# Stick-breaking attention: the mask and 1 - s move from VectorE to GpSimd, and the scores are made two units ahead

## The reference, cut to what matters

```python
def stick_breaking(q, k, v, q_pos, k_pos):
    """A[t,s] = sigmoid(z_ts) * prod_{s<j<t} (1 - sigmoid(z_tj)), s < t, in log space.
    q (B,T,H,d), k/v (B,S,H,d); swept in query blocks."""
    ...
        z = (jnp.einsum('bthd,bshd->bhts', qb, k) * scale).astype(F32)
        mask = k_pos[None, :] < pb[:, None]
        ln1m = jnp.where(mask, jax.nn.log_sigmoid(-z), 0.0)
        rc = lax.cumsum(ln1m, axis=3, reverse=True)
        excl = jnp.concatenate([rc[..., 1:], jnp.zeros_like(rc[..., :1])], axis=-1)
        a = jnp.where(mask, jnp.exp(jax.nn.log_sigmoid(z) + excl), 0.0)
        return jnp.einsum('bhts,bshd->bthd', a.astype(v.dtype), v)
```

## Time and profile before

| | us |
|---|---|
| median of 3 runs | 3688.18 |
| the three runs | 3682.5, 3688.18, 3698.48 |
| profiled execution | 3678.38 |
| its span, first to last instruction | 3676.8 |
| mean granted TensorE clock | 0.929 |

### The profile page before, as it was taken

One profiled execution on the slowest core, in us unless ns is written; L12 is line 12 of the kernel. 1 busy time (PEld: TensorE's weight loads), 2 busy tenths in 40 slices (PEclk: granted clock), 3 DMA queues, 4 the chain that ended last, 5 costly groups with the idle time before them and its releaser, 6 DMA issues. The chain is left out here.

```text
span 3676.8 us, 67694 instructions
## 1 busy us (share of the span) xinstructions
PE 3204.2 (87%) x25256; PEld 1989.8 (54%) x25256; DVE 1365.4 (37%) x3002; ACT 950.5 (26%) x1746; POOL 597.8 (16%) x1090
## 2 busy tenths in 40 slices
PE   6999987888998688799989998978889987887998
PEld 4556654555666455444455666545556654554443
DVE  3235086443224444312142350954433244442211
ACT  2012144332224333211020122433322242331110
POOL 0000000444010044400000000004440101452000
PEclk9999988999999799899989999989999997998999
DMA  5011103887120388710120011048861205995102
GB/s 175 18 36 33 50 10 105 265 287 244 38 83 1 117 278 290 249 66 16 46 96 28 28 45 44 1 129 288 284 217 33 72 1 173 295 299 186 57 29 72
DMA packets 268657, 439.67 MB, mean 120 GB/s; under 512 B 48818, under 2 KB 216403, under 8 KB 268339
## 3 DMA queue, kind: packets, MB, share of 16 engines
q1 hardware_dynamic: 205810, 239.96, 20.4%
q0 software_dynamic: 55744, 189.25, 15.6%
q10 hardware_dynamic: 6912, 7.87, 0.6%
HBM read 410.28 MB, written 26.65 MB: 119 GB/s over the span
## 5 line engine op out<-in xcount | busy, mean ns | idle before, releaser
L806 PE MATMUL ps<-W,xT 128*128 128x320 f32 (+7 forms) x5120 | 1482.9, 465 | 11.5 <-DVEq L449 11.5
L806 PEld LDWEIGHTS ps<-W,xT 128*128 128x128 f32 (+1 forms) x5120 | 856.7, 184 | 585.6 <-issue 291.5
L688 POOL DMA_DIRECT2D branch<-in_cache_sb_v_dram x480 | 258.8, 539 | 637.5 <-issue 597.3
L688 POOL DMA_DIRECT2D branch<-in_cache_fox_v_dram x480 | 258.9, 539 | 621.2 <-issue 579.6
L1468 ACT ACTIVATE branch<-ps 128x512 f32<-128x512 f32 x288 | 165.6, 595 | 386.6 <-PE ps L1051 378.2
L1051 PE MATMUL ps<-C,W 128*128 128x128 f32 x1280 | 199.4, 301 | 73.1 <-DMA W<-in_cache_fox_k_dram 26.6
L1051 PE MATMUL ps<-C,branch 128*128 128x128 f32 x1280 | 194.9, 295 | 65.7 <-DMA branch<-in_cache_sb_k_dram 18.0
L1136 PE MATMUL ps<-branch 128*8 128x64 f32 x9920 | 182.2, 234 | 55.9 <-DMA branch<-in_cache_fox_v_dram 27.6
L1073 PE MATMUL ps<-branch,work 128*32 128x512 f32 x896 | 229.9, 631 | 0.8 <-issue 0.2
L1051 PEld LDWEIGHTS ps<-C,W 128*128 128x128 f32 x1280 | 151.0, 151 | 141.0 <-issue 67.4
L1051 PEld LDWEIGHTS ps<-C,branch 128*128 128x128 f32 x1280 | 147.8, 149 | 146.3 <-issue 96.1
(11 more groups left out here) (246 smaller groups left out, 3389.1 us busy)
## 6 DMA issues: line engine op xcount, KB each, us to landing
branch<-in_cache_sb_v_dram POOLq DMA_DIRECT2D x480, 160.0 KB, 4.3
branch<-in_cache_fox_v_dram POOLq DMA_DIRECT2D x480, 160.0 KB, 4.1
W<-in_cache_sb_k_dram SPq DMA_DIRECT2D x248, 160.0 KB, 3.4
W<-in_cache_fox_k_dram SPq DMA_DIRECT2D x248, 160.0 KB
branch<-in_cache_sb_k_dram SPq DMA_DIRECT2D x240, 160.0 KB, 4.2
branch<-in_cache_fox_k_dram SPq DMA_DIRECT2D x240, 160.0 KB, 4.3
W<-in_w_in_dram SPq DMA_DIRECT2D x14, 1280.0 KB, 6.3
W<-in_w_in_dram SPq DMA_DIRECT2D x9, 1536.0 KB, 7.1
```

The costliest lines, as they stand in the source:

```text
L688: pool.dma_start(ringV[:, g % 2, p * DA:(p + 1) * DA], cache[L, bass.ds(pg, 1)].rearrange("a s h d -> s (a h d)"))\
L806: ins = pe.matmul(out, src[:, k, t * P:t * P + R], W[i % 2][:, k, a:z], start=(k == 0), stop=(k == kc - 1), **place)
```

## The change

DVE's mask and subtraction become instructions of POOL, which now runs a loop over the 40 units in ATT_S: it waits for the sigmoid of u, masks the diagonal block in place, waits for its own mask, from the third unit on for the product of u - 2, and writes 1 - s into one of two buffers. DVE waits for that (att_rest) and is left with scan and product. The second buffer lies in a free part of `branch` at column 7552. In ATT_S the scores are now made two units ahead on PE, and the sigmoid two units ahead on ACT; ATT_F keeps one unit ahead on ACT, and, since PE's loop is shared, two on PE. Two semaphores are new.

```diff
-        rest = branch[:, at + 4 * SEQ:at + 5 * SEQ]
+        rests = [branch[:, at + 4 * SEQ:at + 5 * SEQ], branch[:, 7552:7552 + SEQ]]
...
+        att_cut = sem("att_cut")
+        att_rest = sem("att_rest")
...
                 phase_over(pool, PROJ_S)
+
+                for u, (t, i, h) in enumerate(UNITS):
+                    n = (t + 1) * P
+                    s = sig[:, u % 2, 0:n]
+                    pool.wait_ge(att_first["sb"], u + 1)
+                    pool.tensor_tensor(s[:, t * P:n], s[:, t * P:n], const("before"), ALU.mult).then_inc(att_cut, 1)
+                    pool.wait_ge(att_cut, u + 1)
+                    if u >= 2:
+
+                        pool.wait_ge(att_probs["sb"], u - 1)
+                    pool.tensor_scalar(rests[u % 2][:, 0:n], s, -1.0, 1.0, ALU.mult, ALU.add).then_inc(att_rest, 1)
                 phase_over(pool, ATT_S)
...
                 scores(0)
+                scores(1)
                 for u, (t, i, h) in enumerate(UNITS):
-                    if u + 1 < len(UNITS):
-                        scores(u + 1)
+                    if u + 2 < len(UNITS):
+                        scores(u + 2)
...
                 first(0)
+                ahead = 2 if kind == "sb" else 1
+                if ahead == 2:
+                    first(1)
                 for u, (t, i, h) in enumerate(UNITS):
-                    if u + 1 < len(UNITS):
-                        first(u + 1)
+                    if u + ahead < len(UNITS):
+                        first(u + ahead)
...
-                    r, e = rest[:, 0:n], SEQ - n
-                    dve.wait_ge(att_first[kind], u + 1)
-                    link(dve.tensor_tensor(s[:, t * P:n], s[:, t * P:n], const("before"), ALU.mult))
-                    link(dve.tensor_scalar(r, s, -1.0, 1.0, ALU.mult, ALU.add))
+                    r, e = rests[u % 2][:, 0:n], SEQ - n
+                    dve.wait_ge(att_rest, u + 1)
```

## The result

The changed kernel takes 3646.17 us (median of 4 runs, 3639.03 to 3648.72) beside 3685.34 for the kernel before (4 runs on the same chip): a ratio of 0.9892, 95% interval 0.9871 to 0.9913. So it is about 39 us, 1.1%, faster, where the forecast was 12 us slower. The profiled execution took 3648.39, with a span of 3646.8, 30.0 us under that of before.

The account below looks back on a forecast made before the run. VectorE was taken to bound stick-breaking attention, busy 96% of a steady tile row. Turns at +26 us and forgetting attention at -14 gave +12 on the median of 3688.2: 3700 us, whole range 3640 to 3740.

Parts of the forecast that it names:

- What goes: Stick-breaking attention: 40 masks and 40 subtractions a layer leave VectorE, 33.2 us; scan and product stay, 84.6 us.
- What comes, the price: Stick-breaking attention: masks and subtractions on GpSimd, priced from its nearest rows at 44.9 to 68.3 us a layer.
- cheap end: GpSimd's lower price, taken for the forecast: fixed part plus 0.83 ns a column, 44.9 us a layer.
- rival 3: Stick-breaking attention: engines in turns at GpSimd's dear price, 68.3 us a layer; +50 us in all, 3738 us; chance 0.20.
- rival 4: Stick-breaking attention: GpSimd itself is the bound, needing a fixed cost over 0.5 us; up to 3780 us; chance 0.03.
- Turns: Stick-breaking attention: GpSimd's whole 44.9 us added to VectorE's 84.6; +13 us a layer, +26 in both; chance 0.30.
- rival 2: Stick-breaking attention: turns in part, GpSimd's fixed 0.27 us not holding the path; net -8 a layer, 3658 us; chance 0.16.
- The ring of two units: Stick-breaking attention: product, sigmoid of u + 2, GpSimd, scan, product; 3.0 to 3.5 us a unit, below 4.52 before.
- the copy "hardly late": Stick-breaking attention: ScalarE's copy behind the sigmoid, 1.02 us, is hidden by transposes of 1.97 us at low clock.
- Rival 1: Stick-breaking attention: VectorE and GpSimd side by side, TensorE setting the pace; -14 us a layer, 3646 us in all; chance 0.31.
- ATT_F: Forgetting attention: scores two units ahead shorten the weighing's wait for ScalarE's copy; 7 us a layer, -14 in both.
- rival 5: Where TensorE idles more, its clock may fall to 0.50 in a stretch, such as the phase's last; no term.

## Why the prediction was wrong

- **What goes** (33.2 us a layer): held. Scan and product are all that VectorE has left.
- **What comes, the price** (cheap end): held. Mask 0.41 us for 0.38, subtraction of 1024 columns 1.05 for 1.12. The dear end (rival 3) and GpSimd as the bound (rival 4) are out. The Trainium skill (GPSIMD Engine Reference, 3.1 and 4.1) would have made the mask 0.17 dearer, 0.55 by an estimate from its figure; it is 0.41.
- **Turns**: right as a mechanism, and shown by three runs. **Wrong was its size, and that is the step that failed.** I added GpSimd's whole 44.9 us to VectorE's 84.6, as if an engine that is held up had still everything to do when its turn comes. In the trace only 0.73 us a unit of 768 columns are on the path, where the forecast had 0.38 + 0.91 + 0.10. Two things account for it. The mask is issued in the scan and is done 0.20 us after it; the product beside it takes 0.98 us, and 0.96 where GpSimd is idle, so next to nothing of the mask is on the path. And the subtraction is issued in the product, with its fixed part (0.2 us, by 1.05 at 1024 and 0.83 at 768 columns) behind it when the product ends: what is left then takes 0.70 us, of which 0.64 are the columns. Over the phase VectorE waits 21.8 us for GpSimd and its products are 1.8 us longer (32.1 for 30.3): 23.6 us on its path in place of the forecast's 44.9 + 4.0. That is rival 2, to which I gave 0.16. With its term (net -8 a layer) the time would be 3658; measured was -12 a layer.
- **The finish** was in no case. It took VectorE 0.48 us a tile row. Now it lies in the wait for the subtraction: the scan behind it waits 0.34 us for GpSimd where it waits 0.73 elsewhere. VectorE, layer 0:

```profile
522.91 0.47 DVE L1902 TENSOR_TENSOR O<-O,ps 128x320 f32<-128x320 f32 x1
523.72 1.76 DVE L1875 TENSOR_TENSOR_SCAN branch<-branch 128x768 f32<-128x768 f32 x1 [0.34 <-POOL branch L691]
```

  Some 0.4 us a row, 3 a layer, are hidden so; with them rival 2's -8 comes to -11. That this is near the measured -12 is in part luck: it has nothing of the lead, which alone gives 6.4 and 4.9 us, and it counts VectorE's relief in the first stretch, where it buys nothing. The move by itself, from the run with the lead alone to the changed kernel, is -6.2 and -6.9.
- **The lead in ATT_S** had no term, and this is the second part of what failed: I took 2.2 us off the excess in the first tile row and no gain. The lead gives 5 us in the first stretch (VectorE's wait for the sigmoid, 14.1 to 7.4), the turns take 2.6. I also read that stretch as five units; it holds nine.
- **The ring of two units and the copy "hardly late"**: held. That ATT_S needs the lead, the run without it shows: 22.6 us in one layer and 15.4 in the other.
- **Rival 1** gave 3646, which is the measured median, by the wrong mechanism. That is an accident: its -14 a layer in ATT_S is close to what turns in part with the hidden finish and the lead give (-12), its ATT_F term didn't come, and the rest is scatter. Where GpSimd only writes the phase takes 120.2 us, 5 less than here. It did name the next bound rightly: there TensorE is busy 17.00 of 17.00 us.
- **ATT_F** (-14 in both layers): the mechanism held, in size too, and yet the gain is nearly nil. The row of 18.81 lost 1.72 us (forecast 1.7), the short ones with a full clock 1.04 and 0.67 (14.18 to 13.14, 11.96 to 11.29, read where the clock was kept; forecast 0.7), the first stretch is 41.9 for 44.4; and the weighing's waits on TensorE, 18.0, are 1.6 (forecast 11). Part of them has moved: TensorE's scores now wait 7.1 us for the exponential, so 8.7 are left in all. At the full clock that is some 8 us a layer. But in all 16 profiled ATT_F phases that had the lead from their start the clock was 0.88 in the row of 14.7 us, and this and the rows behind gave back most of what the first ones had gained: the 16 phases have a mean of 130.1 us, the 8 profiled ones without the lead 131.9.
- **The clock** (rival 5) had "no term", and I looked for it only where TensorE idles more. It fell there too (without lead, 0.50 for a whole row), but in ATT_F it fell behind two rows in which TensorE was busy 16.27 of 17.09 and 14.22 of 15.14 us, and not in the rows next behind where it had been busy 16.25 of 18.81. Gaps may not be the whole of it. Of the 8 phases without the lead, the three with that row at 1.00 fell as well, four or five rows later (to 0.85 or 0.73); the five that had it at 0.92, and 20.4 us long, kept 1.00 up to the last row. No run separates how long the full clock had lasted from how few gaps there were; the cause of the fall stays open.

Of the 30.0 us of the profiled pair 24.5 are ATT_S, 2.0 ATT_F, and 3.5 stretches without an edit. That the medians are 39 apart, and the later comparisons 31, is the scatter of executions around that; I assign no cause to it.

## What to carry to other kernels

When two engines take turns, don't add their busy times: ask, at each handover, which part of the blocked instruction is still to be done when its turn comes. What is issued early can have its fixed part behind it, and short work between two long instructions of the other engine can cost nothing; the first experiment is to run the second engine's instruction twice, which shows the price per column on the path. And a move to another engine makes the chain of a unit longer by one handover even where it makes the busiest engine's work shorter; give it a unit of lead with the move, since without it the same edit cost 45 to 50 us instead of gaining 31 to 39.

## What the hardware showed that I had not expected

- Blocking isn't paid by whoever comes second alone: the subtraction issued inside a scan ended 0.84 us after it, and pushed the product behind the scan from 1.23 to 1.88 us.
- The records of the blocked engine show its time blocked too, not its work alone: GpSimd's 82.1 us in ATT_S are some 43 us of work, by 0.41 a mask and 0.20 + 0.83 ns a column for a subtraction. GpSimd's busy share of that phase is no measure of how near it is to being the bound.
- A two-input mask of 128 columns takes 0.41 us on GpSimd, 0.29 on VectorE; a subtraction of 1024 columns 1.05 against 0.69. It is slower by four tenths in the one and by half in the other.
- TensorE's clock fell from 1.00 to 0.88 in ATT_F in all 16 phases in which its gaps were closed from the start, and in 15 of them to 0.76 or 0.67 in the next row. A row of 14.18 us became one of 14.71 with the same matmuls. Closing TensorE's gaps was worth some 8 us a layer at the full clock and 1 to 2 with the clock that it got.
